# The up product of the second feed-forward layer as seven products of halves

## The chip, the cores and the metric

The kernel runs on one core of a Trainium2 chip. TensorE (PE) multiplies matrices and accumulates in PSUM banks; ScalarE (ACT), VectorE (DVE) and GpSimd (POOL) work elementwise; SyncE (SP) issues the DMAs that bring weights from device memory. Each engine runs its own list of instructions in order, and semaphores tie the lists together. The metric is the device time of one execution in microseconds (us), lower is better.

## The reference, cut to what matters

A small network in float32: two layers of one kind (a first block), then two of another (a second block). The change touches the feed-forward part of the first block's second layer, which works on 256 tokens and 1024 channels, `D_FF` = 2816:

```python
def conv_ffn(h, w_up, conv_w, conv_b, w_down):
    u = h @ w_up                       # 256 x 1024 @ 1024 x 5632
    u = depthwise_conv_width_3(u, conv_w) + conv_b   # along the tokens
    a, g = jnp.split(u, 2, axis=-1)
    return (jax.nn.silu(g) * a) @ w_down
```

A norm with modulation stands ahead of it, and the second block with its own feed-forward layer (`swup`, 256 tokens, the same widths) and a mixture of experts behind it.

## The kernel before

Activations lie with channels on the partitions: a tile of 128 channels by all tokens, eight such tiles (`k`) for 1024 channels. Weights stream through `ring`, four slots of 1 MB; a unit is one slot, and `unit_done` counts units that TensorE has finished, which lets SyncE load the next into the slot. The up product of a layer has 22 units, each giving one pair of 128-channel tiles, a half of `a` and a half of `g`.

There are two forms of a unit:

- Direct (`fm_unit`, called by `pairs` for `up1`): two tiles, eight float32 matmuls of 128x256 each, into two of the banks 0 to 3. `lin_free` frees the banks.
- Seven products (`seven_unit`, called by `seven` for `up0` and `swup`): the 1024x256 weights of a unit are cut in quarters of halves by halves, and so are the activations; seven products of half size and sums before and behind them take the place of eight. GpSimd makes four weight sums of 128x512 for each unit (`w_sums`), two units ahead: `sums_ahead(j)` waits until unit j is done and then sums for unit j+2. VectorE makes four sums of the activations once (`x_sums`), and from each unit's PSUM banks the four result quarters with five additions (`c_sums`), after ScalarE has copied the first product out (`seven_head`). The result lies in `Y`, in SBUF. TensorE may begin unit j+2 when `c_sums(j)` is done (`sv_c`), and its third product needs the weight sums (`sv_s`). With 256 tokens a product is 128 tokens wide and each matmul is cut in two strips of 64 columns (`strips`).

Behind a unit of `up1` comes `conv_ffn` on three engines. ScalarE takes the centre tap of both tiles into `CONV` (`SC`, line 1238). VectorE adds the two outer taps of both tiles with four scalar_tensor_tensor (line 1805), in two pairs with a wait on itself in between. ScalarE takes silu of the second tile (line 1242) and increments `lin_free`. GpSimd multiplies the two tiles into `PROJ` (line 2128) and increments `ffn_hid`, for which ScalarE waits before it overwrites `CONV` two units later. In `up0` the taps read `Y`; in `up1` they read the PSUM bank.

On ScalarE the loop over four units starts with a load of the activation table, and the first silu in it loads one too. `down` starts when `lin_free` says that all silus but the last of the layer are done, takes the first 11 of the 22 hidden tiles, and waits for the last `ffn_hid` before the second 11.

Ahead of `up1` stand `wout1` (four units), `norm(5)` with `residual(5)` on VectorE (line 1577 scales a tile of `Y`, line 1580 adds it to `X`, both in SBUF), `norm(6)`, whose squares ScalarE takes from `X` (line 1159) and whose means TensorE makes (line 511), then `modulate(6)` and the modulation on ScalarE (line 1175). On GpSimd nothing stands between the last bias DMA of the attention and the first gating product.

## Time and profile before

| | |
|---|---|
| median of 3 runs | 3517.01 us (3512.43 to 3519.14) |
| the profiled execution | 3511.37 us, its span 3509.5 us |
| TensorE busy | 3358.9 us, 96% of the span |
| VectorE, ScalarE, GpSimd busy | 868.3, 692.6, 432.5 us |
| `up1`: first matmul to the first of `down1` | 1192.14 to 1346.80 us |
| DMA | 637.80 MB, mean 182 GB/s |

In the rows below "idle before <-X" is the time for which an engine stood still before an instruction, and X what ended it. Each float32 matmul leaves two records.
### The profile page before, as it was taken

The numbers are of one execution on the slowest core, as the hardware profiler recorded it, in microseconds if no ns is written. First come the engines' busy times: TensorE is split into PE (matmuls) and PEld (weight loads), VectorE is DVE, ScalarE is ACT, GpSimd is POOL, SyncE is SP. The second block draws the span as 40 slices with busy tenths as digits, with TensorE's granted clock in tenths as the row PEclk, the third lists the DMA queues.
The fourth block names the chain that finished last, engine by engine and source line by source line (L and its number), as shares of the span: only waits on it lengthen the run. The fifth ranks groups of instructions, "written<-read, shape, count | busy, mean of one in ns | idle before, by whom it ended". The sixth has DMA issues, their size and how long they took to land.

```text
span 3509.5 us, 81384 instructions
## 1 busy us (share of the span) xinstructions
PE 3358.9 (96%) x34930; PEld 2919.0 (83%) x34931; DVE 868.3 (25%) x1957; ACT 692.6 (20%) x1501; POOL 432.5 (12%) x393
## 2 busy tenths in 40 slices
PE   7998789999999999999999999979999999999998
PEld 5885678884586788787899887779999999988898
DVE  2325745550214221213232114220100010011000
ACT  2324132220104331212121112211111111111011
POOL 1310125540021000100074100000000000000000
PEclk9999689999899999999999999989999999999999
DMA  6546012222133244333344443339999999944477
GB/s 270 192 162 229 3 48 93 86 69 82 65 112 123 96 153 138 128 121 114 127 163 151 143 142 108 112 128 369 377 354 350 368 378 351 369 158 151 141 278 267
DMA packets 94776, 637.80 MB, mean 182 GB/s; under 512 B 10784, under 2 KB 11824, under 8 KB 38592
## 3 DMA queue, kind: packets, MB, share of 16 engines
q1 hardware_dynamic: 92048, 627.58, 49.0%
q0 software_dynamic: 2608, 8.49, 0.8%
q8 instruction: 91, 1.49, 0.2%
q14 instruction: 29, 0.24, 0.0%
HBM read 634.98 MB, written 1.05 MB: 181 GB/s over the span
## 4 chain that ended last, share of the span: by engine, by line
PE 93%; DVE 2%; ACT 2%; issue 2%; DMA 1%; POOL 0%; SPq 0%; DVEq 0%; ACTq 0%
PE bank L994 20%; PE bank L666 18%; PE bank L608 18%; PE bank L563 12%; PE bank L687 5%; PE bank L579 5%; PE bank L954 2%; PE bank L511 2%; PE bank L537 1%; PE bank L723 1%; PE bank L1009 1%; PE bank L705 1%; PE bank L712 1%; PE bank L1062 1%; ACT H L1175 1%
## 5 line engine op out<-in xcount | busy, mean ns | idle before, releaser
L666 PE MATMUL bank<-PROJ,ring 128*64 128x96 f32 (+2 forms) x7776 | 663.1, 282 | 1.1 <-DMA ring<-in_moe_down 1.0
L666 PEld LDWEIGHTS bank<-PROJ,ring 128*64 128x64 f32 (+1 forms) x7776 | 545.4, 147 | 116.8 <-issue 84.7
L994 PE MATMUL bank<-MIX,ring 128*64 128x96 f32 x12544 | 521.3, 247 | 7.8 <-issue 7.8
L994 PEld LDWEIGHTS bank<-MIX,ring 128*64 128x64 f32 x12544 | 520.0, 137 | 9.7 <-issue 9.7
L563 PE MATMUL bank<-H,ring 128*128 128x256 f32 x1856 | 408.1, 383 | 3.4 <-ACT H L1175 3.3
L563 PEld LDWEIGHTS bank<-H,ring 128*128 128x128 f32 x1856 | 354.9, 192 | 56.1 <-issue 4.7
L994 PE MATMUL bank<-H,ring 128*128 128x256 f32 x896 | 193.7, 379 | 0.0
L608 PE MATMUL bank<-H,ring 128*64 128x128 f32 (+1 forms) x1296 | 185.1, 331 | 5.5 <-ACT H L1175 4.8
L994 PEld LDWEIGHTS bank<-H,ring 128*128 128x128 f32 x896 | 170.2, 190 | 23.4 <-issue 0.3
L608 PE MATMUL bank<-MIX,ring 128*64 128x128 f32 (+1 forms) x1272 | 181.2, 321 | 0.8 <-DVE MIX L1748 0.8
L687 PE MATMUL bank<-H,ring 128*128 128x256 f32 x768 | 177.9, 389 | 3.9 <-ACT PROJ L1264 3.7
L1951 DVE TENSOR_TENSOR PROJ<-SC,bank 128x96 f32 (+1 forms) x224 | 61.6, 275 | 477.4 <-ACT SC L1389 473.2
L608 PEld LDWEIGHTS bank<-H,ring 128*64 128x64 f32 (+1 forms) x1296 | 154.2, 165 | 28.6 <-ACT H L1175 7.2
L687 PEld LDWEIGHTS bank<-H,ring 128*128 128x128 f32 x768 | 147.9, 196 | 28.2 <-issue 7.7
L608 PEld LDWEIGHTS bank<-MIX,ring 128*64 128x64 f32 (+1 forms) x1272 | 147.6, 161 | 19.2 <-issue 4.1
L579 PE MATMUL bank<-ring,H 128*128 128x256 f32 x704 | 158.8, 388 | 2.8 <-ACT PROJ L1191 1.7
L579 PEld LDWEIGHTS bank<-ring,H 128*128 128x128 f32 x704 | 136.4, 195 | 25.3 <-issue 5.7
L1389 ACT ACT_TABLE_LOAD x61 | 78.3, 1283 | 327.0 <-PE bank L994 304.4
L1389 ACT ACTIVATE SC<-bank 128x96 f32<-128x96 f32 (+1 forms) x224 | 60.0, 268 | 415.2 <-PE bank L994 414.6
L2107 POOL TENSOR_TENSOR PR<-ring 128x512 f32<-128x512 f32 x31 | 39.8, 1282 | 639.9 <-DMA ring<-in_swup 270.2
L1805 DVE SCALAR_TENSOR_TENSOR SC<-Y,par,SC 128x510 f32<-128x510 f32 x88 | 98.3, 1157 | 45.5 <-ACT SC L1238 42.5
L2092 DVE TENSOR_TENSOR X<-X,bank 128x512 f32<-128x512 f32 x28 | 19.3, 688 | 304.4 <-PE bank L1062 304.4
(345 smaller groups left out, 3437.3 us busy)
## 6 DMA issues: line engine op xcount, KB each, us to landing
ring<-in_moe_up SPq DMA_DIRECT2D x224, 1024.0 KB, 4.9
ring<-in_moe_down SPq DMA_DIRECT2D x128, 896.0 KB, 6.0
ring<-in_up SPq DMA_DIRECT2D x44, 1024.0 KB, 4.8
ring<-in_mod_b SPq DMA_DIRECT2D x40, 1024.0 KB, 6.2
ring<-in_tproj SPq DMA_DIRECT2D x32, 1024.0 KB, 4.8
ring<-in_proj SPq DMA_DIRECT2D x26, 1024.0 KB, 4.8
ring<-in_gates SPq DMA_DIRECT2D x24, 1024.0 KB, 4.8
ring<-in_down SPq DMA_DIRECT2D x32, 704.0 KB, 4.0
```

Of the source, the lines that this page charges most:

```text
L511: mm = pe.matmul(B[7][:, c:c + 1], H[:, k, c * P:(c + 1) * P], mean_d[:, 0:1], start=first and c == 0, stop=last, skip_group_check=True)
L563: mm = pe.matmul(B[(tile + t) % 4][:, 0:width], w[:, k, t * P:(t + 1) * P], src[:, k, 0:width], start=k == 0, stop=k == k_n - 1)
L579: mm = pe.matmul(B[b0 + (tile + t) % 4][:, 0:2 * P], H[:, k, t * P:(t + 1) * P], w[:, k, :], start=k == 0, stop=k == KT - 1)
L608: mm = pe.matmul(B[bank[0]][lo:lo + m, at:at + n], left[:, k, lo:lo + m], right[:, k, :], start=k == 0, stop=k == 3)
L666: mm = pe.matmul(B[bank][lo:lo + m, 0:width], w[:, k, lo:lo + m], src(s * half + k), start=s == 0 and k == 0, stop=s == 1 and k == half - 1)
L687: mm = pe.matmul(gate_bank(i)[:, 0:T], w[:, k, (i % 2) * P:(i % 2 + 1) * P], H[:, k, 0:T], start=k == 0, stop=k == KT - 1)
L954: mm = pe.matmul(B[tile % 4][:, 0:T], w[:, b, k, :], src(k), start=k == 0, stop=k == 3)
L994: mm = pe.matmul(B[(t0 + 2 * j + t) % 4][lo:lo + m, 0:n], w[:, k, t * P + lo:t * P + lo + m], src[:, k, 0:n], start=k == 0, stop=k == KT - 1)
L1389: act.activation(CONV[:, j % 2, 0, 0:width], src, ACT.Silu).then_inc(S("sw_s"), 1)
L1805: ins = dve.scalar_tensor_tensor(out=o, in0=u, scalar=col, in1=o, op0=ALU.mult, op1=ALU.add)
L1951: dve.tensor_tensor(PROJ[:, bass.ds(it * (NSLOT * width) + j * width, width)], g, up, ALU.mult)\
L2107: pool.tensor_tensor(s2, a11, a21, ALU.subtract).then_inc(S("sv_w"), 1)
```

## The change

`up1` joins the products that are made in the seven-product form, with 256 tokens, as `swup` has it. GpSimd makes its weight sums: two units' ahead of the layer, once `wout1` is done, the others in `conv_ffn`. VectorE makes the sums of the activations and of the results, the taps then read `Y` in SBUF in place of a bank, and for this layer VectorE also makes the gating product, of unit j-1 behind the taps of unit j (`gated`).

```diff
-SEVEN = ('proj0', 'wout0', 'up0', 'proj1', 'swup')
+SEVEN = ('proj0', 'wout0', 'up0', 'proj1', 'up1', 'swup')
@@ tensor
-            pairs("up1", T, ("norm6_out", 0, 1))
+            seven("up1", "norm6_out")
@@ scalar, conv_ffn
                 def pair(j, it):
-                    if name in SEVEN: ... else:
-                        act.wait_ge(unit_done, it * NSLOT + (u0 + j + 1))
+                    c = seven_parts(name, j)[0]
+                    seven_head(name, j, it)
+                    seven_done(name, j, it)
@@ vector, conv_ffn
+                    c_sums(name, j, it)
                     dve.wait_ge(S("conv_c"), it * NSLOT + (l * FT + j + 1))
...
+                            u = flat(seven_parts(name, j)[0][:, 2 * t:2 * t + 2, :])
...
+                def gated(j, it):
+                    dve.wait_ge(lin_free, it * (2 * NSLOT) + (t0 + 2 * j + 2 + 4))
+                    dve.tensor_tensor(PROJ[:, bass.ds(it * (NSLOT * width) + j * width, width)], CONV[:, j % 2, 0, 0:width],
+                                      CONV[:, j % 2, 1, 0:width], ALU.mult).then_inc(S("ffn_hid"), 1)
+
+                loops, peel = FT // NSLOT, FT % NSLOT
+                for j in range(peel):
+                    pair(j, 0)
+                    if l == 1 and j > 0:
+                        gated(j - 1, 0)
                 with dve.Fori(0, loops) as it:
-                    for j in range(NSLOT):
+                    for j in range(peel, peel + NSLOT):
                         pair(j, it)
+                        if l == 1:
+                            gated(j - 1, it)
+                if l == 1:
+                    gated(FT - 1, 0)
@@ vector, the order of the stages
             modulate(6, T)
+            x_sums("up1", "norm6_out")
             conv_ffn(1, T)
@@ gpsimd
                 def pair(j, it, ahead):
-                    if ahead and name in SEVEN:
+                    if ahead:
                         sums_ahead(name, j, it)
-                    pool.wait_ge(lin_free, ...)
-                    pool.tensor_tensor(PROJ[...], ...)
+                    if l == 0:
+                        pool.wait_ge(lin_free, ...)
+                        pool.tensor_tensor(PROJ[...], ...)
@@ gpsimd, the order of the stages
+            pool.wait_ge(unit_done, base["wout1"] + 4)
+            w_sums("up1", 0)
+            w_sums("up1", 1)
             conv_ffn(1, T)
```

## Rows read from the trace of the kernel before

**Rows 1.** The page, part 1: busy time, share of the span, count.

```profile
PE 3358.9 (96%) x34930; PEld 2919.0 (83%) x34931; DVE 868.3 (25%) x1957; ACT 692.6 (20%) x1501; POOL 432.5 (12%) x393
```

**Rows 2.** Chain of waits, in time: start us, us, what it was.

```profile
1192.14 154.65 PE bank L563 x704
1346.80 13.38 PE bank L666 x62
```

**Rows 3.** Windows: attention, norms, up1: busy times, PEclk, DMA share, GB/s.

```profile
1092.00:1150.00 58.00, 51.09 (x454) 32.84 (x452) 41.91 (x143) 43.38 (x102) 15.06 (x28) 1.00 0.46 146
1178.00:1192.00 14.00, 9.98 (x51) 9.10 (x49) 6.81 (x22) 5.12 (x14) 0.00 (x0) 0.70 0.23 76
1216.00:1346.00 130.00, 130.00 (x604) 114.42 (x604) 33.20 (x76) 37.38 (x65) 13.79 (x19) 1.00 0.43 146
```

**Rows 4.** Timeline, one direct unit of up1: start us, us, engine, line.

```profile
1326.32 1.02 ACT L1238 ACTIVATE SC<-bank,par 128x256 f32<-128x256 f32 x2 [3.33 <-PE bank L563]
1327.48 1.89 DVE L1805 SCALAR_TENSOR_TENSOR SC<-bank,par,SC 128x255 f32<-128x255 f32 x4 [5.01 <-ACT SC L1238]
1329.48 0.42 ACT L1242 ACTIVATE SC<-SC 128x256 f32<-128x256 f32 x1 [2.14 <-DVE SC L1805]
...
1333.22 1.02 ACT L1238 ACTIVATE SC<-bank,par 128x256 f32<-128x256 f32 x2 [3.33 <-PE bank L563]
```

**Rows 5.** Timeline, a seven-product unit of swup, 256 tokens.

```profile
1875.75 0.42 DVE L1783 TENSOR_TENSOR Y<-Y,bank 128x256 f32<-128x256 f32 x1 [1.00 <-PE bank L608]
...
1878.37 0.29 DVE L1774 TENSOR_TENSOR Y<-Y,bank 128x128 f32<-128x128 f32 x1 [1.02 <-PE bank L608]
...
1881.87 0.42 DVE L1783 TENSOR_TENSOR Y<-Y,bank 128x256 f32<-128x256 f32 x1 [1.00 <-PE bank L608]
1881.91 1.28 POOL L2107 TENSOR_TENSOR PR<-ring 128x512 f32<-128x512 f32 x1 [0.72 <-PE bank L608]
...
1882.40 0.42 ACT L1389 ACTIVATE SC<-Y 128x256 f32<-128x256 f32 x1 [5.49 <-DVE Y L1783]
1882.74 0.28 ACT L1183 ACTIVATE Y<-bank 128x128 f32<-128x128 f32 x1
```

**Rows 6.** Timeline of up0, 512 tokens: taps from Y beside the weight sums.

```profile
661.48 2.42 DVE L1805 SCALAR_TENSOR_TENSOR SC<-Y,par,SC 128x510 f32<-128x510 f32 x2 [1.91 <-ACT SC L1238]
661.63 1.73 POOL L2111 TENSOR_TENSOR VT<-ring 128x512 f32<-128x512 f32 x1
```

**Rows 7.** Timeline of up0, VectorE and GpSimd, the same taps' second part.

```profile
662.15 1.76 DVE L1805 SCALAR_TENSOR_TENSOR SC<-Y,par,SC 128x510 f32<-128x510 f32 x1
663.44 1.59 POOL L2113 TENSOR_TENSOR VT<-ring,VT 128x512 f32<-128x512 f32 x1
```

**Rows 8.** Timeline ahead of swup: a VectorE sum of 256 columns beside GpSimd.

```profile
1747.49 1.27 POOL L2111 TENSOR_TENSOR PR<-ring 128x512 f32<-128x512 f32 x1
1747.56 1.48 DVE L1553 TENSOR_TENSOR H<-H 128x256 f32<-128x256 f32 x1 [0.48 <-ACT H L1159]
1748.83 1.32 POOL L2113 TENSOR_TENSOR PTB<-ring,PR 128x512 f32<-128x512 f32 x1
...
1751.01 0.42 DVE L1553 TENSOR_TENSOR H<-H 128x256 f32<-128x256 f32 x1 [0.48 <-ACT H L1159]
```

**Rows 9.** Timeline of up0 behind the taps: silu, copy of the first product, first sum.

```profile
642.17 0.63 ACT L1242 ACTIVATE SC<-SC 128x512 f32<-128x512 f32 x1 [5.00 <-DVE SC L1805]
642.71 0.37 ACT L1183 ACTIVATE Y<-bank 128x256 f32<-128x256 f32 x1
...
643.19 0.42 DVE L1774 TENSOR_TENSOR Y<-Y,bank 128x256 f32<-128x256 f32 x1 [1.13 <-ACT Y L1183]
```

**Rows 10.** Groups by line in up1, shapes apart: busy us, mean ns.

```profile
L1242 ACT ACT_TABLE_LOAD x5 | 6.4, 1283 | 10.7 <-DVE SC L1805 10.7
```

**Rows 11.** Timeline of the norms ahead of up1.

```profile
1181.59 0.42 DVE L1580 TENSOR_TENSOR X<-X,Y 128x256 f32<-128x256 f32 x1
...
1185.59 0.75 DVE L1580 TENSOR_TENSOR X<-X,Y 128x256 f32<-128x256 f32 x2
1186.05 0.75 ACT L1159 ACTIVATE H<-X 128x256 f32<-128x256 f32 x2 [0.25 <-DVE X L1580]
```

**Rows 12.** Timeline of TensorE in the norms ahead of up1.

```profile
1182.52 6.61 PE L511 MATMUL bank<-cst,H 128*128 128x1 f32 x32 [1.63 <-ACT H L1159]
```

**Rows 13.** Timeline at the end of up1.

```profile
1350.26 0.73 POOL L2128 TENSOR_TENSOR PROJ<-SC 128x256 f32<-128x256 f32 x1 [6.18 <-ACT SC L1242]
```

More of the change, by code:

```diff
@@ L28 @@
 MOD_A = 8
-SEVEN = ('proj0', 'wout0', 'up0', 'proj1', 'swup')
-SEVEN_UNITS = {'proj0': 11, 'wout0': 4, 'up0': 22, 'proj1': 4, 'swup': 22}
-SEVEN_WIDTH = {'proj0': 512, 'wout0': 512, 'up0': 512, 'proj1': 512, 'swup': 256}
+SEVEN = ('proj0', 'wout0', 'up0', 'proj1', 'up1', 'swup')
+SEVEN_UNITS = {'proj0': 11, 'wout0': 4, 'up0': 22, 'proj1': 4, 'up1': 22, 'swup': 22}
+SEVEN_WIDTH = {'proj0': 512, 'wout0': 512, 'up0': 512, 'proj1': 512, 'up1': 256, 'swup': 256}
 MOD_P = 22
@@ L409, in seven_parts @@
             n, q = SEVEN_WIDTH[name] // 2, seven_at(name) + j
-            if name in ("up0", "swup"):
+            if name in ("up0", "up1", "swup"):
                 at = 6 * T * (q % 2)
@@ L585, in wout @@
                     fm_unit(base[name] + j, tile_base[name] + 2 * j, src, width, ready=ready if j == 0 else None, half=True)
-            def pairs(name, width, ready):
-                u0, t0, peel = base[name], tile_base[name], FT % NSLOT
-                for j in range(peel):
-                    fm_unit(u0 + j, t0 + 2 * j, H, width, ready=ready if j == 0 else None)
-                with pe.Fori(0, FT // NSLOT) as it:
-                    for j in range(peel, peel + NSLOT):
-                        fm_unit(u0 + j, t0 + 2 * j, H, width, it, 2 * NSLOT)
             def seven_unit(name, j, it=0, ready=None, tight=False, between=None):
@@ L1236, in pair @@
                         col = lambda w: cw[:, bass.ds(it * (4 * NSLOT) + 4 * (t * FT + j) + w, 1)]
-                        src = flat(c[:, 2 * t:2 * t + 2, :]) if name in SEVEN else B[(t0 + 2 * j + t) % 4][:, 0:width]
+                        src = flat(c[:, 2 * t:2 * t + 2, :])
                         mm = act.activation(CONV[:, j % 2, t, 0:width], src, ACT.Identity, bias=col(3), scale=col(1))
@@ L1792, in pair @@
                 def pair(j, it):
-                    if name in SEVEN:
-                        c_sums(name, j, it)
+                    c_sums(name, j, it)
                     dve.wait_ge(S("conv_c"), it * NSLOT + (l * FT + j + 1))
@@ L2134, in conv_ffn @@
                         pair(j, it, True)
-                for j in range(loops * NSLOT, FT):
-                    pair(j, 0, False)
+                if l == 0:
+                    for j in range(loops * NSLOT, FT):
+                        pair(j, 0, False)
             def window_means(l):
```

22 lines of the change are left out of this document (4 added, 18 removed).

## Prediction, made before the changed kernel was run

> **What bounds the kernel now.** I read the page first: TensorE is busy for 3358.9 of 3509.5 us [rows 1]. A stage gets shorter only if TensorE gets its work done sooner there, and longer if anything else falls behind TensorE. Then the chain of waits around the change: `up1` is one unbroken piece of TensorE work of 154.65 us, and `down1` follows without a gap [rows 2]. The stretch of the windows that lies within it says the same, TensorE 130.00 of 130.00 us at clock 1.00, VectorE 33.20, ScalarE 37.38 and GpSimd 13.79 [rows 3]. So the other engines have room on average. Whether they have it within one unit is read from the timelines of one unit of each form. A direct unit takes 1333.22 - 1326.32 = 6.90 us [rows 4]; a seven-product unit at 256 tokens takes 1881.87 - 1875.75 = 6.12 us in `swup` [rows 5]. But `swup` has no taps: VectorE's and ScalarE's part of a unit is small there. `up0` has taps, but at 512 tokens its unit is twice as long while the GpSimd sums are of the same size. No stage of the kernel before has taps, weight sums and a unit as short as 6.12 us together; that stage has to be put together from rows.
>
> **The change part by part.**
>
> TensorE. 22 units of 6.90 become 22 of 6.12: 22 x 0.78 = 17.2 us less, if nothing else is late. The first unit is its own case, worked out below.
>
> GpSimd's own time. Before the unit that starts at 1881.91 it had been idle for 0.72 of the 6.1 us, so four sums with their waits take 5.4 us [rows 5]. The gating product leaves it. It fits under 6.12 by 0.7 us if undisturbed.
>
> The chain of one unit through ScalarE and VectorE. In program order: last addition of `c_sums(j)`; centre taps on ScalarE; four outer taps on VectorE; silu on ScalarE; `seven_head(j+1)` behind it on ScalarE; `c_sums(j+1)` on VectorE. Nothing of this may be reordered, since each engine keeps its list. Priced at 256 tokens: from the last addition's start to ScalarE's start 1882.40 - 1881.87 = 0.53 [rows 5]; centre taps 1.02 and 0.14 to the taps, taps 1.89, 0.11 to silu [rows 4]; silu to the copy 1882.74 - 1882.40 = 0.34, the copy 0.28 [rows 5], 0.11 to the first sum [rows 9]; the four additions ahead of the last, of which L1774 is one at 0.29, two more are as wide as it and one as wide as L1783 at 0.42 [rows 5], 3 x 0.29 + 0.42 = 1.29. Sum: 0.53 + 1.02 + 0.14 + 1.89 + 0.11 + 0.34 + 0.28 + 0.11 + 1.29 = 5.71 us. `gated(j-1)` lies beside silu and copy (0.73) and costs nothing as long as it takes less. That is 0.4 below the 6.12 of TensorE: the chain would keep up.
>
> Table loads. Each turn of ScalarE's loop has a load ahead of the copy and one ahead of the first silu, 1.28 us each [rows 10]. Before, they lay beside TensorE; now they lie in the chain. From unit 0 to unit 21 nine of them do: 9 x 1.28 = 11.5 us, or 0.55 per unit: the chain needs 6.26 on average, 0.14 more than TensorE.
>
> The taps beside the weight sums. This term decides. The taps now have two SBUF inputs, `Y` and `SC`, where one was a bank. `up0` shows what such a tap does beside a weight sum. The first tap runs from 661.48 and the second starts at 662.15; the sum issued at 661.63 takes 1.73 instead of 1.27, the second tap takes 1.76 and ends at 663.91, 0.55 behind that sum's end at 663.36; the next sum, issued at 663.44, is longer by 0.32 [rows 6, 7]. So they take turns, a whole instruction each: a tap that meets a weight sum waits for all that is left of it, and a weight sum already waiting goes ahead of the next tap. At 256 columns the same is seen once ahead of `swup`: a VectorE addition takes 1.48 instead of 0.42 and ends 0.28 behind the GpSimd sum's end, 1748.76 [rows 8]. GpSimd loses little: 1.32 for 1.27.
>
> How much per unit, called E. Below: 0, if the four taps always met an idle GpSimd; above, if each tap waited for a whole sum, 4 x 1.27 = 5.1 less what runs side by side. For a value I walk through one unit in the state that sets in when the chain is slower than TensorE. Then TensorE starts unit j+2 when `c_sums(j)` ends, finishes it 6.2 later, and GpSimd's sums start there. With a chain of some 7.6 us per unit that is 2 x 7.6 - 6.2 = 9.0 ahead of the end of `c_sums(j+2)`, or, one turn on, 1.4 ahead of the end of each `c_sums`. From that end (0): sums at -1.4 to -0.1, 0.0 to 1.2, third from 1.3; first tap issued at 0.1 + 1.02 + 0.14 = 1.3, waits to 2.5, ends 2.8; fourth sum to 4.0; second tap 4.2; GpSimd is done; third and fourth taps to 5.1. Taps 1.3 to 5.1 = 3.8 where 1.89 stood: E = 1.9. Then the turn is 5.71 + 1.9 = 7.6, which closes the circle. The first few units, where GpSimd starts right at the end of the unit, meet three sums and lose about 2.6; units with a table load meet fewer. I take E = 1.9, for the 19 turns in which GpSimd has sums to make (the last two have none), and the range has 1.0 (a tap loses against one sum only) to 2.6.
>
> The Trainium skill's page "SBUF — State Buffer", section "Who interferes with whom", says the same kind of thing: a VectorE instruction with two SBUF inputs and a GpSimd instruction that reads SBUF exclude each other, and issue order decides. The trace agrees on the exclusion, 1.48 us for 0.42 [rows 8]. By its order alone the second tap at 662.15 would wait behind the sum of 661.63, as it does [rows 6, 7]; the sum would come out at the same value.
>
> The start of the layer. GpSimd now runs eight sums from 1178.2 on, to about 1189, and VectorE's eight additions `X + Y`, both in SBUF, run in that time, from 1181.59 at a pitch of 0.67 to 1186.34 [rows 11]. Taking turns by the rule above, the first six end behind a sum each (1182.5, 1184.0, 1185.4, 1186.9, 1188.3, 1189.7), the last at 1190.8, which is 4.4 later. The squares follow 0.46 behind [rows 11]. TensorE's means ended at 1189.13, paced by TensorE, 2.3 behind the squares, four records being 0.83 [rows 12]; two tiles' means behind the late squares end at 1192.5: +3.4 us on the path. Between 0 (they don't meet) and 4.4.
>
> The first unit. TensorE is held by the modulated tiles for 3.5 us, its clock low, 0.70 in the norms before [rows 3]; two of seven products by then, one at the low clock, four at 0.87: it ends 8.7 behind its start. Start 1192.1 + 3.4 = 1195.5, end 1204.2.
>
> The sum. From the first unit's end: last addition 0.5; 21 turns of 5.71 = 119.9; table loads 11.5; 19 x 1.9 = 36.1; then the tail of unit 21: 0.11 + 1.02 + 0.14 + 1.89 + 0.11 + 0.42 + 0.1 + 0.43 = 4.2. Together 172.2: the last gated tile is there at 1376.4. The loads overlap with E in part, so I take off 1: 1375.4. Before, it was there at 1350.99 [rows 13], and TensorE reached the second half of the first down tile, which needs it, at about 1351.5, as 11 matmuls of 0.43 stand before it from 1346.80 on [rows 2]. So `down1` goes on at 1375.5 instead of 1351.5: +24.0 us. TensorE itself is done with `up1` some 9 us before, waits for the silu of unit 20 and fills 4.75 us of that with the first 11 matmuls. Behind that, nothing changes: SyncE's loads are early, and GpSimd has no later sum that these could delay. On the profiled execution of 3511.4 this gives 3535.4; that execution lies 5.6 below the median of 3517.0, and on the median the forecast is 3541.
>
> **The rivals.**
>
> They keep out of each other's way. The chain could settle so that the taps fall behind the fourth sum, into the time in which GpSimd waits for the next unit (0.72 per unit in `swup`, more if units are longer), and E is near 0. The chain then ends at 1204.2 + 0.5 + 119.9 + 11.5 + 4.2 = 1340.3, 11.2 us ahead of 1351.5: 3506 on the median, faster. It decides from E = 0.6 down, where 19 x E is 11. For it: a chain that falls behind shifts against GpSimd's sums. Against: four taps need 1.9 us, the gap is 0.7 as long as units are short, and rows 6 to 8 each show VectorE waiting for most of a sum.
>
> VectorE wins the port and GpSimd becomes the bound. Five VectorE instructions with two SBUF inputs each hold GpSimd up by 0.3 (the 0.32 of the second sum in [rows 7]): four sums take 5.4 + 1.5 = 6.9, a unit 7.0 with the wait for `unit_done`. 1204.2 + 21 x 7.0 + 0.5 + 4.2 = 1355.9, +4 us: 3521, the same within what can be told. For it: GpSimd's sums were stretched too in [rows 6, 7]. Against: by 0.05 only at 256 columns [rows 8].
>
> TensorE's clock falls. In the forecast TensorE is busy for about 80% of the stretch, in pieces of 6.1 and gaps of 1.5 us. In the attention, at 51.09 of 58.00 us, the clock stayed 1.00; in the norms, at 9.98 of 14.00, it was 0.70, the one level for part of the time [rows 3]. If it fell in a third of the units, each of these taking 12.2 instead of 6.1 against a chain of 7.8, that is 7 x 4.4 = 31 us more, less what its slack takes: 3560. The skill's page "TensorE: Matmul & The Clock Gate", section "What's actually happening", calls the low level the default and activity what releases it; no row here shows at which share of idle time it returns.
>
> **How the numbers follow.** Forecast 0.74: 3541. Its own range takes the bounds: E = 1.0 is 19 x 0.9 = 17 less, 3524, and with no delay of the norms 3521; E = 2.6 is 13 more, 3554, and 3556 with 4.4 for the norms and some of the clock's loss. Out of each other's way: 0.12, 3506. GpSimd the bound: 0.08, 3521. Clock: 0.06, 3560. The range leaves out the first and the last of the rivals: 3518 to 3557. A change of 0.2% (7 us) is about the least that can be told here from none: below 3510 faster, above 3524 slower. Faster 0.13, same 0.09 (the third case and the low end of the first), slower 0.78.
>
> **What would show it.** In the profile after: taps (L1805 of before) with `Y` as source at a mean near 0.9 us against 0.48; units of `up1` 7.5 to 8 us apart instead of 6.12; TensorE idle before matmuls of the seven form, ended by VectorE's `Y`; the weight sums hardly longer than 1.3; means ahead of `up1` some 3 us later; TensorE waiting at the start of `down1`. It is wrong if the taps stay under 0.6, if units are 6.1 apart, or if TensorE waits for GpSimd's sums instead.

## The result and the profile after

| | before | after |
|---|---|---|
| median | 3516.02 us of 4 runs (3512.43 to 3519.14) | 3551.47 us of 4 runs (3551.04 to 3553.05) |
| profiled execution, its span | 3511.37, 3509.5 us | 3551.57, 3549.7 us |
| from the first `X + Y` addition to the first matmul of `up1` | 10.55 us | 14.55 us |
| from there to the first output tile of `down1` | 164.19 us | 192.68 us |

The change makes the kernel 35.5 us slower: the ratio of the times is 1.0102, with a 95% interval of 1.0088 to 1.0116. The forecast was 24 us slower, 3541 in a range of 3518 to 3557.

Line numbers move by 6 to 17: the taps (1805 before) are now line 1788, `X + Y` (1580) is 1567, centre tap and silu (1238, 1242) are 1225 and 1229, the copy of the first product (1183) is 1174, the sums of results (1774 to 1783) are 1761 to 1770, the weight sums (2107 to 2113) are 2101 to 2107, the matmuls of the seven form (608) 599, those of `down` (666) 657, and the gating product is 1797. Here is the page's first part, which answers [rows 1]:

```profile
PE 3363.2 (95%) x36690; PEld 2935.3 (83%) x36691; DVE 957.9 (27%) x2093; ACT 698.9 (20%) x1523; POOL 533.2 (15%) x459
```

No engine but TensorE is busy for a third of the span, and yet TensorE waits. The groups by line within `up1` (1195 to 1385 us, shapes apart; the columns are busy us, mean ns, and the idle time ahead with what ended it) show for whom:

```profile
L1788 DVE SCALAR_TENSOR_TENSOR SC<-Y,par,SC 128x255 f32<-128x255 f32 x88 | 76.4, 908 | 35.5 <-ACT SC L1225 32.5
L599 PE MATMUL bank<-H,ring 128*64 128x128 f32 x704 | 54.3, 318 | 27.6 <-DVE Y L1770 26.4 <-ACT H L1166 1.2
L2103 POOL TENSOR_TENSOR ring<-ring 128x512 f32<-128x512 f32 x20 | 25.9, 1293 | 1.6
L2105 POOL TENSOR_TENSOR PR<-ring 128x512 f32<-128x512 f32 x10 | 13.3, 1330 | 0.8
L1797 DVE TENSOR_TENSOR PROJ<-SC 128x256 f32 x20 | 8.5, 425 | 4.7 <-DVE SC L1788 4.7
```

A tap has a mean of 908 ns where four of them took 1.89 us [rows 4], TensorE stands still for 26.4 us until VectorE's last addition, and the weight sums are hardly longer than alone. One unit, as VectorE, ScalarE and GpSimd run it, is in the timeline (start, duration; merged lines span all of their instructions):

```profile
1248.98 1.27 POOL L2103 TENSOR_TENSOR ring<-ring 128x512 f32<-128x512 f32 x1
1249.27 4.50 DVE L1788 SCALAR_TENSOR_TENSOR SC<-Y,par,SC 128x255 f32<-128x255 f32 x4 [1.49 <-ACT SC L1225]
1250.33 1.34 POOL L2105 TENSOR_TENSOR PR<-ring 128x512 f32<-128x512 f32 x1
1251.75 1.34 POOL L2107 TENSOR_TENSOR PTB<-ring,PR 128x512 f32<-128x512 f32 x1
1253.87 0.42 ACT L1229 ACTIVATE SC<-SC 128x256 f32<-128x256 f32 x1 [4.74 <-DVE SC L1788]
1253.99 0.42 DVE L1797 TENSOR_TENSOR PROJ<-SC 128x256 f32 x1 [0.23 <-DVE SC L1788]
1255.91 0.42 DVE L1770 TENSOR_TENSOR Y<-Y,bank 128x256 f32<-128x256 f32 x1
1256.47 2.49 PE L599 MATMUL bank<-H,ring 128*64 128x128 f32 x32 [2.30 <-DVE Y L1770]
```

and the same taps in the chain of waits of that window:

```profile
1249.35 1.11 issue
1250.46 1.50 DVE SC L1788
...
1252.18 1.12 issue
1253.29 0.48 DVE SC L1788
```

The four taps take 4.50 us. The tap that begins at 1250.46, 0.13 behind the issue of the sum at 1250.33, lasts 1.50 and ends at 1251.96, which is 0.29 behind that sum's end at 1251.67. The last tap, with GpSimd idle by then, takes 0.48. Three taps each wait for a sum, and 2.30 us of waiting of TensorE follow at 1256.47. The same is seen in `X + Y` ahead of the layer, against [rows 11]:

```profile
1181.95 1.33 POOL L2107 TENSOR_TENSOR PTB<-ring,PR 128x512 f32<-128x512 f32 x1
...
1182.41 1.16 DVE L1567 TENSOR_TENSOR X<-X,Y 128x256 f32<-128x256 f32 x1
1183.24 1.45 POOL L2101 TENSOR_TENSOR VT<-ring 128x512 f32<-128x512 f32 x1
...
1183.82 1.16 DVE L1567 TENSOR_TENSOR X<-X,Y 128x256 f32<-128x256 f32 x1
```

The additions come at a pitch of 1.4 us, that of the sums, where it was 0.67. The windows of `up1`, the start of `down1` and the 60 us behind it, in the form of [rows 3]:

```profile
1206.00:1376.00 170.00, 141.68 (x2318) 139.16 (x2312) 114.41 (x203) 45.53 (x89) 103.94 (x79) 0.92 0.36 124
1376.00:1386.00 10.00, 9.34 (x36) 7.96 (x37) 4.53 (x13) 3.58 (x7) 0.00 (x0) 0.83 0.31 102
1386.00:1446.00 60.00, 60.00 (x280) 52.82 (x279) 2.55 (x6) 5.24 (x14) 0.00 (x0) 1.00 0.45 155
```

TensorE was busy for 130.00 of 130.00 us before [rows 3] and is for 141.68 of 170.00 now.

One thing lies outside the layer. Ahead of the experts' matmuls, 1000 us later, the chain of waits holds two pieces named "issue" around two small matmuls. In the kernel before they are

```profile
2335.57 7.03 issue
2342.59 0.63 PE bank L1022 x2
2343.23 2.91 issue
```

and in the kernel after

```profile
2368.78 11.55 issue
2380.33 0.63 PE bank L1013 x2
2380.96 5.01 issue
```

("issue" is time for which the chain has no releaser.) That is 6.6 us more in a place that the change does not touch. The experiments return to it.

### The profile page after: what moved, and what is told of

It reads as the page before. It is cut to its first block, busy times and chain, and to the rows that moved or that the text cites. A ratio compares the mean times of both kernels' runs of the same rounds, so it can differ in the third digit from the quotient of the medians.

```text
span 3549.7 us, 85440 instructions
## 1 busy us (share of the span) xinstructions
PE 3363.2 (95%) x36690; PEld 2935.3 (83%) x36691; DVE 957.9 (27%) x2093; ACT 698.9 (20%) x1523; POOL 533.2 (15%) x459
## 4 chain that ended last, share of the span: by engine, by line
PE 58%; DVE 3%; issue 3%; ACT 1%; DMA 1%; DVEq 0%; ACTq 0%; SPq 0%
PE bank L985 20%; PE bank L657 13%; PE bank L563 6%; PE bank L678 5%; PE bank L599 4%; PE bank L945 2%; PE bank L579 2%; DVE SC L1788 1%; PE bank L1000 1%; DMA ring<-in_moe_down 1%; PE bank L1053 1%; PE bank L871 1%; PE bank L511 0%; ACT SC L1225 0%; DVE Y L1770 0%
## 5 line engine op out<-in xcount | busy, mean ns | idle before, releaser
L599 PE MATMUL bank<-H,ring 128*64 128x128 f32 (+1 forms) x2000 | 238.7, 326 | 33.4 <-DVE Y L1770 26.4
L563 PE MATMUL bank<-H,ring 128*128 128x256 f32 x1152 | 253.4, 383 | 2.2 <-ACT H L1166 2.1
L599 PEld LDWEIGHTS bank<-H,ring 128*64 128x64 f32 (+1 forms) x2000 | 200.8, 163 | 60.7 <-issue 21.6
L563 PEld LDWEIGHTS bank<-H,ring 128*128 128x128 f32 x1152 | 219.4, 191 | 35.8 <-ACT H L1166 3.4
L599 PE MATMUL bank<-MIX,ring 128*64 128x128 f32 (+1 forms) x1976 | 227.5, 305 | 0.8 <-DVE MIX L1735 0.8
L599 PEld LDWEIGHTS bank<-MIX,ring 128*64 128x64 f32 (+1 forms) x1976 | 188.2, 153 | 19.2 <-issue 4.1
L1788 DVE SCALAR_TENSOR_TENSOR SC<-Y,par,SC 128x510 f32<-128x510 f32 (+1 forms) x176 | 174.6, 1032 | 81.0 <-ACT SC L1225 75.1
L985 PE MATMUL bank<-H,ring 128*128 128x256 f32 x896 | 193.7, 379 | 0.0
L985 PEld LDWEIGHTS bank<-H,ring 128*128 128x128 f32 x896 | 170.2, 190 | 23.4 <-issue 0.3
L678 PE MATMUL bank<-H,ring 128*128 128x256 f32 x768 | 177.2, 388 | 3.9 <-ACT PROJ L1251 3.7
L678 PEld LDWEIGHTS bank<-H,ring 128*128 128x128 f32 x768 | 147.5, 195 | 27.9 <-issue 7.9
L2101 POOL TENSOR_TENSOR PR<-ring 128x512 f32<-128x512 f32 x42 | 54.0, 1287 | 740.9 <-DMA ring<-in_swup 273.8
L1376 ACT ACT_TABLE_LOAD x61 | 78.3, 1283 | 334.0 <-PE bank L985 311.1
L2103 POOL TENSOR_TENSOR ring<-ring 128x512 f32<-128x512 f32 x85 | 110.4, 1299 | 6.7
```

The costliest lines, as they stand in the source:

```text
L563: mm = pe.matmul(B[(tile + t) % 4][:, 0:width], w[:, k, t * P:(t + 1) * P], src[:, k, 0:width], start=k == 0, stop=k == k_n - 1)
L599: mm = pe.matmul(B[bank[0]][lo:lo + m, at:at + n], left[:, k, lo:lo + m], right[:, k, :], start=k == 0, stop=k == 3)
L678: mm = pe.matmul(gate_bank(i)[:, 0:T], w[:, k, (i % 2) * P:(i % 2 + 1) * P], H[:, k, 0:T], start=k == 0, stop=k == KT - 1)
L985: mm = pe.matmul(B[(t0 + 2 * j + t) % 4][lo:lo + m, 0:n], w[:, k, t * P + lo:t * P + lo + m], src[:, k, 0:n], start=k == 0, stop=k == KT - 1)
L1376: act.activation(CONV[:, j % 2, 0, 0:width], src, ACT.Silu).then_inc(S("sw_s"), 1)
L1788: ins = dve.scalar_tensor_tensor(out=o, in0=u, scalar=col, in1=o, op0=ALU.mult, op1=ALU.add)
```

## The experiments

How they are read. Executions differ by some us in stages that lie ahead of the change: the first `X + Y` addition starts at 1181.59 in the profile before, at 1180.89 after, and between 1177.33 (e6) and 1184.36 (e2) over all. So the stage is measured within each trace. S is the time from the first `X + Y` addition to the first matmul of `up1`; P is the 21 turns from the first unit's last addition to that of the last unit; D is the time from the first `X + Y` addition to the first output tile of `down1`, the whole stretch that the change can reach; R is the rest, from the first load of `tproj`, the stage behind `down1`, to the end of the span; G is the sum of the two "issue" pieces. A load of `tproj` comes 52.4 us behind the first tile of `down1` in every kernel (1408.7 - 1356.33 before, 1440.5 - 1388.12 after), so D and R have nothing between them that changes.

| kernel | time, us | tap, ns | S | P | D | R | G |
|---|---|---|---|---|---|---|---|
| before | 3511.37 (profiled) | - | 10.55 | - | 174.74 | 2100.8 | 9.9 |
| after | 3551.47 | 908 | 14.55 | 173.96 | 207.23 | 2109.2 | 16.6 |
| e1 thin sums | 3510.52 | 481 | 10.54 | 135.61 | 165.02 | 2107.7 | 15.1 |
| e12 two sums | 3521.56 | 586 | 12.19 | 145.36 | 175.92 | 2108.5 | 14.9 |
| e5 split sums | 3537.13 | 782 | 11.03 | 162.29 | 193.53 | 2107.6 | 16.5 |
| e2 early sums | 3551.14 | 870 | 10.55 | 170.97 | 200.66 | 2111.7 | 16.1 |
| e7 early copy | 3532.68 | 877 | 14.55 | 161.25 | 194.83 | 2104.6 | 14.7 |
| e6 gating on GpSimd | 3540.92 | 862 | 14.54 | 169.20 | 202.55 | 2106.7 | 15.3 |
| e4 memset | 3512.81 | 482 | 10.92 | 135.66 | 165.72 | 2111.4 | 16.4 |
| e3 results in PSUM | 3505.06 | 478 | 14.55 | 128.31 | 161.35 | 2109.6 | 16.4 |
| e8 the same, sums early | 3501.55 | 479 | 10.54 | 128.31 | 157.77 | 2107.6 | 15.4 |
| e9 before again | 3517.63 | - | 10.54 | - | 174.72 | 2105.6 | 10.2 |
| e10 before, longer code | 3512.75 | - | 10.36 | - | 175.04 | 2100.7 | 10.2 |
| e11 after, longer code | 3541.62 | 870 | 14.55 | 171.03 | 204.78 | 2101.4 | 6.7 |

The time is a median for after, e3 and e8, and of one execution otherwise; the other columns are read from one profiled execution each (3551.57 us for after, 3508.87 for e3, 3500.92 for e8). The kernel before, run beside the experiments, had 3514.29 to 3516.68. The code of `up1` that shapes P is the same in after, e2 and e11, and P is 173.96, 170.97 and 171.03 there: differences in P below 3 us tell nothing.

The theory: VectorE's taps and GpSimd's weight sums, both of which read two operands from SBUF, take turns by whole instructions, and this makes the chain of a unit (from one unit's last addition through ScalarE and VectorE to the next one's) longer than TensorE's unit. The first rival: the chain through ScalarE and VectorE with its table loads is too long by itself. The second: GpSimd's four sums are the bound. The third: TensorE's clock.

### e1: weight sums of almost no size

```diff
                 s0, s1, s2, s3 = (w_sum(u, q, i) for i in range(4))
+                if name == "up1":
+                    a11, a12, a21, a22, s0, s1, s2, s3 = (a[:, :, 0:2] for a in (a11, a12, a21, a22, s0, s1, s2, s3))
```

> The weight sums of up1 are made on 8 of their 512 columns only, so GpSimd is nearly idle there; everything else is as in the changed kernel (the layer's result is not the reference's). Taking turns (each tap loses a whole weight sum): taps at 0.48 us instead of 0.91, the last additions of the units 6.1 to 6.3 us apart instead of 8.3, the additions X + Y of the norm ahead at 0.42 instead of 1.2, TensorE's start of up1 at about 1192; in all about 45 us less than 3551, that is 3503 to 3510. Rival, the chain by its length and its table loads: taps at 0.48, but units still 7.5 or more apart, above 3535. Rival, TensorE's waits and clock: units above 7, the clock near 0.92 in the stretch.

Measured: 3510.52 us beside 3516.68 of before, half a microsecond above the range that was expected. Groups by line in `up1`:

```profile
L599 PE MATMUL bank<-H,ring 128*64 128x128 f32 x698 | 43.7, 279 | 2.3 <-DVE Y L1770 2.3
L1788 DVE SCALAR_TENSOR_TENSOR SC<-Y,par,SC 128x255 f32<-128x255 f32 x88 | 38.7, 481 | 35.4 <-ACT SC L1225 32.5
```

The taps are back at 481 ns with the same operands in `Y`, TensorE waits for 2.3 us in place of 26.4, and D is 42.2 us shorter than after and 9.7 shorter than before. So nothing in the taps' own work is slow, nor in reading `Y`; it is the sums beside them. The first rival keeps a small part: P is 135.61, a pitch of 6.46 where 6.1 to 6.3 was expected, against the 6.11 that TensorE needs (e3 below). The timeline of one unit without a table load shows the chain:

```profile
1236.11 0.42 DVE L1770 TENSOR_TENSOR Y<-Y,bank 128x256 f32<-128x256 f32 x1
1236.79 1.09 ACT L1225 ACTIVATE SC<-Y,par 128x256 f32<-128x256 f32 x2 [2.07 <-DVE Y L1770]
1238.02 1.90 DVE L1788 SCALAR_TENSOR_TENSOR SC<-Y,par,SC 128x255 f32<-128x255 f32 x4 [1.48 <-ACT SC L1225]
1240.03 0.42 ACT L1229 ACTIVATE SC<-SC 128x256 f32<-128x256 f32 x1 [2.15 <-DVE SC L1788]
1240.35 0.26 ACT L1174 ACTIVATE Y<-bank 128x128 f32<-128x128 f32 x1
...
1242.06 0.42 DVE L1770 TENSOR_TENSOR Y<-Y,bank 128x256 f32<-128x256 f32 x1
```

From last addition to last addition it takes 5.95 us (5.92 in the units around it), and 21 x 5.92 = 124.3 leaves 11.3 us for the nine table loads.

### e12: two of the four sums whole

The first two sums of each unit are as in after, the last two as thin as in e1.

```diff
-                pool.tensor_tensor(s1, s0, a11, ALU.subtract).then_inc(S("sv_w"), 1)
-                pool.tensor_tensor(s3, a12, s1, ALU.subtract).then_inc(S("sv_s"), 1)
+                pool.tensor_tensor(s1[:, :, 0:2], s0[:, :, 0:2], a11[:, :, 0:2], ALU.subtract).then_inc(S("sv_w"), 1)
+                pool.tensor_tensor(s3[:, :, 0:2], a12[:, :, 0:2], s1[:, :, 0:2], ALU.subtract).then_inc(S("sv_s"), 1)
```

> Of the four weight sums of a unit of up1 the first two are whole, the last two are made on 8 of 512 columns (the layer's result is not the reference's). With four thin ones units were 6.46 apart and taps 0.48, with four whole ones 8.28 and 0.91. Taking turns: two whole instructions stand in the way at most twice per unit, units 6.9 to 7.5 apart, taps 0.6 to 0.75, about 3525. Rival, the taps are late only once GpSimd has no free time left (a threshold): units below 6.6 apart, 3512.

Measured: 3521.56 us beside 3514.29. A tap has 586 ns and P is 145.36. Over e1 that is 9.75 us, or 0.51 for each of 19 units, where four sums give (173.96 - 135.61) / 19 = 2.02. Half of the sums give a quarter of the delay. The timeline shows why: from 1262 us on, a tap waits for the second sum in three units of four (taps of 0.72, 1.50 and 1.13 us, turn by turn) and never for the first, which is over or nearly so when the taps begin, as in the walk of the prediction. The threshold rival is out: its pitch was to stay below 6.6, and it is 6.92. By D, 175.92, this kernel stands 1.2 us behind the kernel before, 1.6 us of it from the later start (S 12.19 for 10.55): with two sums the turns already cost about what the seven products save.

### e5: each sum in two halves

```diff
+                def one(dst, x, y, op, sem):
+                    if name == "up1":
+                        pool.tensor_tensor(dst[:, 0:2, :], x[:, 0:2, :], y[:, 0:2, :], op)
+                        dst, x, y = dst[:, 2:4, :], x[:, 2:4, :], y[:, 2:4, :]
+                    pool.tensor_tensor(dst, x, y, op).then_inc(S(sem), 1)
-                pool.tensor_tensor(s2, a11, a21, ALU.subtract).then_inc(S("sv_w"), 1)
+                one(s2, a11, a21, ALU.subtract, "sv_w")
```

> Each weight sum of up1 (512 columns) is cut in two instructions of 256, the same work. Taking turns by whole instructions: a tap waits at most for half as long, the mean of a tap falls from 0.91 to 0.65 to 0.75, units 7.2 to 7.7 apart instead of 8.3, 3530 to 3542. Rival, the two engines share the port by rate: the taps stay at 0.9, units 8.3 or more apart, since GpSimd has more instructions, 3551 or more.

Measured: 3537.13 us beside 3516.68. GpSimd computes the same and is busy for longer (552.3 us in the page, 533.2 after), yet the taps take 782 ns for 908, `X + Y` has a mean of 0.63 us where most of these additions took 1.16, and D is 13.7 us shorter. The gain is a little smaller than expected, which was 0.65 to 0.75 us for a tap and a pitch of 7.2 to 7.7 (it is 7.73). Timeline of one unit:

```profile
1268.06 2.86 DVE L1788 SCALAR_TENSOR_TENSOR SC<-Y,par,SC 128x255 f32<-128x255 f32 x4 [1.55 <-ACT SC L1225]
1268.59 0.79 POOL L2103 TENSOR_TENSOR VT<-ring,VT 128x256 f32<-128x256 f32 x1
1269.34 0.91 POOL L2105 TENSOR_TENSOR VT<-ring,VT 128x256 f32<-128x256 f32 x1
```

If the two engines shared a rate, it would be the sum of the work that counts, and splitting would gain nothing. That it gains means that what a tap waits for is the instruction in front of it: the two engines take turns.

### e2: the first two units' sums early

The wait for `wout1` in front of them is taken out; the sums then need only the weights, and run during the attention's end.

```diff
-            pool.wait_ge(unit_done, base["wout1"] + 4)
             w_sums("up1", 0)
```

> The weight sums of the first two units of up1 no longer wait for the end of wout1, but run as soon as their weights are there, beside wout1. Taking turns: VectorE's additions X + Y meet no GpSimd sum, 0.42 each, and the first matmul of up1 comes 3.5 to 4 us sooner, near 1191.5 instead of 1195.4; within up1 nothing changes; 3547 to 3549 in all. Rival, the norms are paced by TensorE's means at the low clock: start as before within 1 us, 3551.

Measured: 3551.14 us beside 3516.68. `X + Y` is at 0.42 again and S at 10.55, exactly as before the change: the start of the layer costs 4.00 us in after and nothing here. The stage's time D is 6.6 us shorter, 4.0 of it in S; P is 3.0 shorter too, which no edit of e2 touches and e11 shows as well. The whole time does not show it, since this execution was 3.5 us late before the first `X + Y` addition (1184.36 for 1180.89) and had 2.5 us more in R. So the expected 3547 to 3549 was missed; one execution can't tell such a gain, the trace can, and the medians of e3 and e8 below, which differ by this edit alone, do (3505.06 and 3501.55).

### e7: the copy of the next unit's first product ahead of silu

```diff
                     mm.then_inc(S("conv_c"), 1)
+                    if l == 1 and not (j == FT - 1 and isinstance(it, int)):
+                        seven_head(name, j + 1, it)
                     act.wait_ge(S("conv_d"), it * NSLOT + (l * FT + j + 1))
```

> ScalarE copies the first product of unit j+1 out ahead of its wait for the taps of unit j, instead of behind the silu. That takes silu, copy and both table loads off the chain, about 0.7 us per unit and 11.5 us for the loads; the taps keep their waits. Chain bound: units 7.2 to 7.6 apart instead of 8.3, 3528 to 3538. Rival, the port alone sets the pace (four sums of 1.27 and five VectorE instructions in turn): units stay near 8, above 3545.

Measured: 3532.68 us beside 3516.68, D 12.4 shorter than after, P 161.25. With the copy out of the chain a turn is 0.60 us shorter, 7.68 where 7.2 to 7.6 was expected; the taps' mean hardly moves, 877. So a shorter chain helps, but the taps still wait for the sums. The expectation took both table loads off the chain; half of them have only moved, in this kernel to the front of the centre taps (x5 at 1283 ns, with 14.5 us of waiting for VectorE's `Y` ahead of them).

### e6: the gating product back on GpSimd

The `gated` calls go out of VectorE's list, and GpSimd's `pair` makes the product behind the sums, as in the kernel before.

```diff
-                    if l == 0:
+                    if True:
                         pool.wait_ge(lin_free, it * (2 * NSLOT) + (t0 + 2 * j + 2 + 4))
```

> The gating product of up1 goes back to GpSimd, behind the weight sums of each unit as in up0; the rest is as in the changed kernel. GpSimd then cannot start the sums of the next unit before the silu of this one, which ties them to ScalarE and VectorE: taps still meet two to three sums. Taking turns: units 7.8 to 8.6 apart, 3540 to 3560, with TensorE also waiting for GpSimd's sums. Rival, the product on VectorE is what makes the chain late: units below 7.5 apart, under 3535.

Measured: 3540.92 us beside 3514.29; D is 4.7 us shorter than after. Here TensorE does wait for GpSimd. Its waits in `up1` (engine, line, for what, us in total, times, longest) are

```profile
PE bank L599 <- POOL VT L2101: 17.3, 10, 2.5
PE bank L599 <- POOL PTB L2101: 6.0, 6, 1.4
PE bank L599 <- DVE Y L1770: 3.5, 4, 0.9
```

while in after they are

```profile
PE bank L599 <- DVE Y L1770: 26.4, 10, 3.8
```

But the second rival, GpSimd bound by its own work, is not true here either. GpSimd stands still for 47.8 us in `up1`, 2.2 a unit, each time ahead of its product and until ScalarE's silu, and silu waits for the taps. Its sums are late because the product ties it to the same chain. The move of the product to VectorE buys nothing in this stage, though: the taps have nearly the same mean, 862, and the pitch is 8.06 for 8.28.

### e4: memsets in place of the sums

Each sum becomes an addition of two columns and a memset of 384 columns, so that GpSimd writes but hardly reads.

```diff
+                        pool.tensor_tensor(s[:, 0:1, 0:2], a[:, 0:1, 0:2], a[:, 0:1, 0:2], ALU.add)
+                        pool.memset(s[:, 1:4, :], 0.0).then_inc(S("sv_s" if i == 3 else "sv_w"), 1)
```

> In up1 each weight sum is replaced by a sum of two columns and a memset of 384 columns, so that GpSimd writes SBUF but reads next to nothing (the layer's result is not the reference's). If only reads of SBUF exclude each other: taps that lie beside a memset stay at 0.48, units 6.2 to 6.5 apart, 3506 to 3514, as in e1. If every GpSimd access to SBUF holds the port: taps beside a memset are longer by the rest of it, units 6.6 or more apart.

Measured: 3512.81 us beside 3515.26. The taps have 482 ns, D is 165.72 and P 135.66, as in e1. The taps do meet memsets, which take 417 ns each: by the timeline 27 of the 88 taps and 5 of the 22 gating products lie beside memsets for over 0.2 us. Each of these taps takes 477 to 486 ns and each of these products 0.42 to 0.43 us, as alone, and no memset takes over 0.42. One meeting, of a gating product with both inputs in SBUF:

```profile
1238.70 0.42 POOL L2104 MEMSET PR<- 128x384 f32 x1
...
1238.91 0.43 DVE L1797 TENSOR_TENSOR PROJ<-SC 128x256 f32 x1 [0.23 <-DVE SC L1788]
```

It starts 0.21 before the memset ends and takes 0.43, its undisturbed time. So a GpSimd instruction that only writes SBUF doesn't hold VectorE up; what excludes in this kernel is GpSimd's reading. The Trainium skill's page "SBUF — State Buffer", section "Who interferes with whom", says that a VectorE instruction with two SBUF inputs contends with a GpSimd instruction that reads SBUF, and not with one that only writes. The trace agrees.

### e3: the results in a PSUM bank

The last additions write to a free bank instead of `Y`. Two of the four result quarters take part in further additions and still pass through `Y`. Centre tap and outer taps then read the bank. TensorE waits for the first sum of results before it reuses the bank, and e7's early copy is in it.

```diff
+            if name == "up1":
+                return B[4 * (j % 2) + 3][:, :].rearrange("p (i t) -> p i t", t=P)
...
-                dve.tensor_tensor(d[:, 0, :], e[:, 1, :], both[0][:, 0, :], ALU.add)
+                dve.tensor_tensor(out[:, 0, :], e[:, 1, :], both[0][:, 0, :], ALU.add)
...
-                            u = flat(seven_parts(name, j)[0][:, 2 * t:2 * t + 2, :])
+                            u = flat(seven_result(name, j)[:, 2 * t:2 * t + 2, :])
```

> The last additions of up1 write the four result quarters into a PSUM bank instead of Y (two products share a bank to free one), so that the taps again read a bank and SC, one SBUF input each; ScalarE copies the first product early, as in e7. GpSimd's weight sums are unchanged. Taking turns: taps at 0.48 although GpSimd is as busy as before; only the gating product can still wait; units 6.1 to 6.3 apart, the first matmul of down1 near 1341; 3500 to 3510, below the kernel before. Rival, GpSimd's being busy beside VectorE slows the taps whatever they read: taps above 0.7, 3530.

Measured over 9 runs: 3505.06 us (3500.87 to 3509.62) against 3515.26 of before; ratio 0.9972 with an interval of 0.9962 to 0.9982. Groups by line in `up1`:

```profile
L1806 DVE SCALAR_TENSOR_TENSOR SC<-bank,par,SC 128x255 f32<-128x255 f32 x88 | 38.4, 478 | 40.1 <-ACT SC L1238 37.2
L2121 POOL TENSOR_TENSOR ring<-ring 128x512 f32<-128x512 f32 x20 | 25.4, 1270 | 1.6
L1815 DVE TENSOR_TENSOR PROJ<-SC 128x256 f32 x20 | 11.4, 572 | 4.7 <-DVE SC L1806 4.7
```

GpSimd does the whole of its work, and the taps take 478 ns, although 77 of the 88 lie beside a weight sum for over 0.2 us (the longest takes 485 ns). Against e7, the same kernel but for the place of the results and what that needs of banks and waits, that is 33 us less in P and D. Only the gating product, with two SBUF inputs still, is stretched to 572, and it is off the chain. P is 128.31, a pitch of 6.11, TensorE's own: against [rows 3] TensorE is busy for 119.00 of 119.00 us between 1206 and 1325 again. Within these 21 turns TensorE is the bound again.

### e8: results in PSUM and the first sums early

e3 with e2's edit.

> e3 and the early weight sums of e2 together. Taking turns: the first matmul of up1 3 to 4 us sooner than in e3, 3497 to 3507, the fastest version. Rival, the start is paced by the modulated tiles and the low clock, so that the first unit ends where it did: the same as e3 within 1 us.

Measured over 7 runs: 3501.55 us (3498.99 to 3504.57) against 3515.26; ratio 0.9965 with an interval of 0.9953 to 0.9976. It beats both kernels. Timeline of one unit:

```profile
1246.52 1.89 DVE L1806 SCALAR_TENSOR_TENSOR SC<-bank,par,SC 128x255 f32<-128x255 f32 x4 [1.41 <-ACT SC L1238]
1246.60 1.27 POOL L2123 TENSOR_TENSOR VT<-ring 128x512 f32<-128x512 f32 x1
1247.95 1.28 POOL L2125 TENSOR_TENSOR VT<-ring,VT 128x512 f32<-128x512 f32 x1
1248.65 0.86 DVE L1815 TENSOR_TENSOR PROJ<-SC 128x256 f32 x1 [0.23 <-DVE SC L1806]
```

Four taps run beside two sums, and neither is any longer than alone, 1.89 as in [rows 4] and 1.27. The gating product at 1248.65 waits for the sum and ends 0.28 behind it: the two sorts of VectorE instruction side by side. D is 157.77, 17.0 us less than before; the 22 x 0.78 = 17.2 us that TensorE was to save are all there.

### e9 to e11: the stretch ahead of the experts

Over after, e12 and e1 to e8 D goes from 157.77 to 207.23, and G stays at 14.7 to 16.6 us where before has 9.9. So G doesn't follow from the time that `up1` takes, nor from what GpSimd and VectorE do there. What they share is the seven form of `up1`, whose code on TensorE is longer. e9 is the kernel before once more, for the scatter. e10 writes out two of the five turns of TensorE's loop over four units in the kernel before, e11 one turn in the kernel after; neither changes any work. In records of the trace e10's eight units are 256 matmuls and 256 weight loads, e11's four are 448 and 448.

```diff
@@ e10, pairs
+                peel += 2 * NSLOT
-                with pe.Fori(0, FT // NSLOT) as it:
+                with pe.Fori(0, FT // NSLOT - 2) as it:
@@ e11, seven
+                turns = FT // NSLOT
+                if name == "up1":
+                    for j in range(peel, peel + NSLOT):
+                        seven_unit(name, j)
+                    peel, turns = peel + NSLOT, turns - 1
```

> The kernel before once more, for the two stretches without a named cause ahead of the experts (7.03 and 2.91 us in its first profile, 11.5 to 11.7 and 3.0 to 5.0 in eight kernels of the seven form). If they belong to the code's place: 7.0 and 3 to 5 again. If they are chance: anything between 6 and 12.

> The kernel before, with two of the five turns of TensorE's loop over the units of up1 written out, so that TensorE's program is longer by 256 matmuls and weight loads and nothing else changes. If the longer wait ahead of the experts (7.03 and 2.91 before, 11.6 and 3.0 to 5.0 in every kernel of the seven form so far) comes with the length or place of TensorE's code: 10 us or more in sum 11 to 16 there, 3519 to 3523. If it comes with the seven form itself or is chance: 7 and 3 as before, 3512 to 3519.

> The changed kernel with one of the five turns of TensorE's loop in up1 written out, which makes TensorE's program longer by 224 matmuls and as many weight loads. Within up1 nothing changes. If the stretch ahead of the experts depends on where TensorE's code lies: other than 11.6, up or down. If it belongs to the changed programs of the other engines: 11.6 as before. In all 3545 to 3557.

Measured: e9 3517.63, e10 3512.75, e11 3541.62 us. e10 moves G by nothing (6.33 and 3.87, beside 6.86 and 3.29 in e9). e11 moves it by 10 us; its chain of waits has

```profile
2366.88 2.00 issue
2368.88 0.63 PE bank L1018 x2
2369.51 4.65 issue
```

in place of 11.55 and 5.01. Its R is 2101.4, that of the kernel before, 7.8 under that of after, and D is 2.4 under it; the time is 9.9 us less. By its expectation e10 alone would have said that G belongs to the seven form or to chance; e11, the seven form with 2.00, shows that it doesn't. How much code stands on TensorE ahead of the first piece decides its length there, with the same work. That the change moved it in the same way is argued from this, not shown, and e10, which had more code too, shows that longer isn't simply better or worse.

The traces also hold the fetches of instructions, in blocks of 16 KB. In the kernel after, the view of DMA has for the first piece, 2368.8 to 2380.3,

```profile
DMA packets 0, 0.00 MB, mean 0 GB/s; under 512 B 0, under 2 KB 0, under 8 KB 0
```

and for the second, 2380.3 to 2385.97,

```profile
q8 instruction: 1, 0.02, 1.5%
```

## Why the prediction was right and where it was wrong

**What bounds the kernel, and TensorE's gain.** Right. A seven unit takes 6.11 us in e3 and e8 where 6.12 was read in `swup` [rows 5], and e8 gains the whole 17 us.

**GpSimd's own time.** Right: four sums fit within a unit of 6.11 (e8), and TensorE never waits for them in after. In e6 it does, but because GpSimd waits for silu and not for want of time.

**The chain without the sums, 5.71 us.** Too low by 0.21. e1 has 5.92: from the last addition's start to ScalarE's 0.68 us where 0.53 was taken from `swup` [rows 5], and the centre taps 1.09 from `Y` where 1.02 was the time from a bank [rows 4]. Over 21 turns that is 4.4 us. The nine table loads came to 11.3 for 11.5.

**The taps beside the sums, E.** The mechanism was right, in the form in which [rows 6 to 8] show it: whole instructions in turn, GpSimd losing little. E was put at 1.9; it is 2.02 in after and (170.97 - 135.61) / 19 = 1.86 in e2, which has the same code in this stage, and in e11. The 1 us taken off for table loads that overlap was not there: turns with loads are the longest in after, at up to 10.9 us between last additions. In after, 19 x 0.12 = 2.3 and that 1 are 3.3 us.

**The start of the layer.** +4.0, forecast +3.4, bounded by 4.4. The additions take turns as drawn; S is 10.55 or 14.55, and e2 and e8 give all of it back. The first unit then took 8.72 us for 8.7.

**The end of the layer.** The last gated tile was forecast for 1375.4 and came at 1382.7, which is 1383.4 counted from the first `X + Y` addition as before. TensorE had 11 matmuls to do before it needed that tile. They took 6.51 us where they took 4.75 before, at a granted clock of 0.83 between 1376 and 1386 after a wait of 2.59 us, and ended at 1383.17, 0.46 behind the tile. From there to the first tile of `down1` it is 4.95 us in both kernels. So the low level cost some 0.4 us, and with 0.1 by which the old time, 1351.38, lay below the 1351.5 of the prediction this is +0.5.

**The sum.** Within the stage: 0.6 for the start, 4.2 for the chain and its loads (4.4 less 0.2), 3.3 for E, 0.5 for the end, with the last steps 0.1 shorter than drawn, 8.5 in all. D grew by 32.5 us where 24.0 was forecast, 8.5 more. The term within the stage that was furthest off is the 5.71, a small error of one turn multiplied by 21. The mechanism is the forecast one, so the direction and most of the size are no luck. That the time still lies in the range partly is: the upper part of the range was made for an E of up to 2.6, and what filled it were the chain (4.4 us) and a stretch that was put at nothing.

**"Behind that, nothing changes."** Wrong. In R after has 8.4 us more than the profiled execution of before. Against the mean of before, e9 and e10 (2102.4) the ten seven-form kernels with TensorE's loop as it is have 2108.5, 6.1 more, and their mean G is 15.7 against 10.1, 5.6 more. So nearly the whole of it is in the stretch ahead of the experts; e11 points to the place of TensorE's code, and no wait of the change reaches there. D and this make 32.5 + 5.6 = 38.1; the medians differ by 35.5. The 2.6 between them is of the size by which executions of one kernel differ in R (before 2100.8, e9 2105.6).

**The rivals.** "They keep out of each other's way" is out: E does not settle near 0, though the chain did shift against the sums as drawn. It would have been worth what e1 shows. "VectorE wins and GpSimd is the bound" is out: the weight sums are hardly stretched, and even in e6 GpSimd has time to spare. "The clock falls" is half true: the windows have 0.92 in `up1`, with single sixteens of matmuls at 1.98 in place of 1.04 us after a wait, but it costs nothing there, since TensorE waits for VectorE again afterwards; e7 has 1.00 over 1206 to 1325, with TensorE busy for 99.80 of 119.00 us, and its taps still wait.

## What to carry to other kernels

Before an operand moves from PSUM to SBUF, or work is given to GpSimd, count on the chain of one unit the VectorE instructions that have both inputs in SBUF: each can cost what is left of a whole GpSimd instruction, 1.5 us for 0.48 here, however idle both engines are by their shares. The remedy is in the operands (one input from a PSUM bank, free of cost here) or in the size of the GpSimd instructions, and where neither goes, in making GpSimd's work at another time. And a term of a chain that recurs 21 times has to be read for the very pair of instructions that will stand there: 0.21 us of it came to 4.4 us, more than the error in E, which was argued at length. A stretch far from the change should be compared too before the whole difference is put down to the change: some 6 of the 35.5 us lay there.

## What the runs showed of the hardware

The gap on TensorE ahead of the experts was not expected. It ends at two matmuls whose input had long been made, has no releaser in the trace, and lasted 7.03, 6.86 and 6.33 us in the three kernels with the direct form, 11.45 to 11.67 in the ten with the seven form, and 2.00 in the one with a loop turn written out. It is followed by a piece of 2.9 to 5.0 us that ends 2.09 to 2.19 us behind the landing of a 16 KB block of instructions, in all fourteen kernels. The Trainium skill's page "Runtime: NRT & Kernel Launch", section "Instruction fetch mechanics", says that an engine reads its code in blocks, and that a taken branch to a block that isn't there stalls until it is fetched. The trace agrees for this second piece, which lies where the source has TensorE branch to the code of an expert (`pe.If(dense)`). It doesn't for the first, in which no block is fetched; with the alignment as a candidate its cause stays open. Nor was e11's edit tried together with e8, where by G it might bring up to 9 us more.

The other is how steady the turns are. S is 10.54 or 10.55 us without large sums beside it in five kernels (10.36 in e10; 10.92 in e4, where the additions aren't longer) and 14.54 or 14.55 with them in five others: the disturbance is not noise, and the prediction had it to 0.6 us. Half sums (e5) make it 11.03, two whole of four (e12) 12.19.
